# Pairing the levels of a gated recurrence: two levels per step in column halves of one PSUM bank

## The chip, the cores and the metric

The kernel runs on one core of a Trainium2 chip. Its five engines each follow their own instruction stream: TensorE (PE; its weight loads are listed apart as PEld), VectorE (DVE), ScalarE (ACT), GpSimd (POOL) and SyncE (SP), which here only issues transfers. Streams are tied together by semaphores. The metric is device time in microseconds; lower is better.

## The reference, cut to what matters

Two model blocks run one after the other on a sequence of 512 tokens and width 2048. The second one has two branches that are computed side by side: a "rw" branch with 16 heads of 64, and a gated "hg" branch with 8 heads of 128. The change is in the gated branch, and a small part of it in the rw branch. Per head of the gated branch:

```python
b = jnp.cumsum(lf_c, axis=1)
diff = b[:, :, None] - b[:, None, :]
decay = jnp.where(causal, jnp.exp(jnp.where(causal, diff, 0.0)), 0.0)
att = jnp.einsum('btshd,bshd->btsh', q_c[:, :, None] * decay, k_c)
o_intra = jnp.einsum('btsh,bshv->bthv', att, i_c)
o_inter = jnp.einsum('bthd,bhdv->bthv', q_c * jnp.exp(b), S)
```

`att[t, s]` is the sum over the 128 channels d of q[t, d] * k[s, d] * exp(b[t, d] - b[s, d]) for s <= t: a causal product whose decay depends on the channel.

## The kernel before, in words

**Levels.** The kernel works in chunks of 128 tokens, 4 chunks for 512 tokens. The decay is made safe by levels: level lv (0 to 6) covers the pairs (t, s) whose positions differ first in bit lv, with t in the odd and s in the even half of a block of 2^(lv+1) tokens. For each level the reference point is the last token of the even half. `level_in` (VectorE, two operations) subtracts, `level_exp` (ScalarE) exponentiates, `level_mix` (VectorE, two operations, L1866 and L1867) multiplies the odd halves by q and the even halves by k into the buffer `mix[lv % 2]`. The product of that buffer with its own odd columns, 4 matmuls (one a chunk) of 128 channels, up to 128 output partitions and 64 columns (L1428), gives the level's part of `att`. It goes to PSUM bank 7, and a masked copy on VectorE (`keep_where`, L1251) takes it to `att` in SBUF. The eighth product, `hk` with `hqs` with 128 columns, gives the diagonal. After each copy the next product may overwrite the bank.

**Rows.** `level_rows` leaves away weight columns at the end that no pair needs: 127, 126, 124, 120, 114, 98, 66 for levels 0 to 6, and 128 for the diagonal.

**The order of the work.** Every engine walks through the same blocks of weights. A block is 8 slots (of 2 x 128 rows of the weights), a slot 8 points, and at each point TensorE does three products with 512 columns, which are the large matrix products (L281 to L283 where the weights are the stationary side, L285 to L287 in the output projection). ScalarE (L576) and VectorE (L744) split each slot's weights into a high and a low part, two slots ahead. The steps of the two branches are hung up at points: `hg_at(h, m)` gives the point of step m of head h, `rw_at(u, k)` that of the rw branch. Steps of heads 0 to 5 are 4.5 points apart, those of head 6 are 2.3 and those of head 7 are 2.0. TensorE runs a step exactly at its point; ScalarE and VectorE run those of a slot's first half before the split and those of the second half after it.

**Steps of the gated branch.** Steps 0 to 6 prepare q, k, the decay sums and the first two levels. At step m from 7 to 13 VectorE mixes level m - 7, and from 7 to 11 prepares level m - 5; from step 8 to 15 TensorE multiplies level m - 8 (step 15: the diagonal) and VectorE, after its mix, copies the product out. Step 17 turns `hkd`, steps 18 to 21 go through the chunks, 24 turns the output.

**Bank 7.** `D_USES` says which steps of the two branches use bank 7 and how many releases each needs; they are numbered in program order. `d_claim` makes TensorE wait until all earlier uses are released (semaphore `d_free`), `d_wait` makes the reader wait for the product (`d_done`). The rw branch uses it too, for four products a unit, among them the turn of its output (L1292, step END + 3).

**The rw branch.** It inverts triangular matrices of 128 in levels too. In levels 4 and 5 a step multiplies in quadrants of 64 x 64 (`level_halves_pe`): W (L1378) and T (L1381), 16 matmuls each, the two diagonal quadrants in turn. Their results for T are copied with a mask by VectorE in `chunk_dve`. The last level has T in the form of L1397.

fp32 matmuls appear in the trace as two records each, so 4 matmuls are x8. The first attention, far ahead of these branches, has products of 128 input partitions with 64 output partitions in two column halves (L338); they are named below as rows of the trace.

## Time and profile before

| | us |
|---|---|
| median of 3 runs | 3055.62 (3054.82 to 3061.11) |
| the profiled execution | 3057.21 |
| its span | 3055.1 |
| TensorE busy | 2950.8 |
| VectorE busy | 1702.6 |
| ScalarE busy | 1187.0 |

The span is the time from the first to the last instruction; the execution's own time has some 2 us around it. "Busy" of TensorE counts overlapping records once. A row of the timeline gives the start and the time to the last end of a run of like instructions; as matmuls overlap, what a group costs TensorE is read from the starts of its neighbours. An idle time is given in brackets with what ended it. The granted clock is a share of 2.4 GHz: 1.00, or 0.50 for 1.2 GHz.

### The profile page before, as it was taken

To read this page: it belongs to the slowest core of one execution; us is meant where nothing else is said; L and a number is where in the kernel's file an instruction comes from. 1 tells how busy PE (TensorE), PEld (TensorE's weight loads), DVE (VectorE), ACT (ScalarE), POOL (GpSimd) and SP (SyncE) were. 2 spreads that over 40 slices of the span, in tenths; PEclk is the share of its full clock that TensorE was granted. 3 is DMA by queue.
4 is the path that set the end of the run, shared out by engine and by line. 5 is a ranking of instruction groups with operands and counts; after the bars stand their busy time and mean duration, and the time that the engine had idled before them with its cause. 6 is when DMAs were issued, how large, how long until landed. Compare 5 with 4: busy or idle time off the path is not lost.

```text
span 3055.1 us, 40093 instructions
## 1 busy us (share of the span) xinstructions
PE 2950.8 (97%) x15738; PEld 2359.3 (77%) x15738; DVE 1702.6 (56%) x2961; ACT 1187.0 (39%) x2099; POOL 285.5 (9%) x517
## 2 busy tenths in 40 slices
PE   8999999999999999999999999999999999999897
PEld 6778777787878887777778877777777877867686
DVE  6554555545453336566653365657666666565647
ACT  5444343434332323333333333434544343434412
POOL 0110101001000000000000002202022020212001
PEclk9999999999999999999999999999999999999899
DMA  4222222222233322222233322212222131225334
GB/s 167 76 83 80 80 83 83 76 83 77 83 121 135 122 92 70 77 70 75 71 123 138 117 86 82 82 66 92 75 73 92 63 99 59 89 77 153 125 132 157
DMA packets 86010, 289.02 MB, mean 95 GB/s; under 512 B 12208, under 2 KB 12720, under 8 KB 85568
## 3 DMA queue, kind: packets, MB, share of 16 engines
q1 hardware_dynamic: 69696, 243.65, 23.4%
q0 software_dynamic: 16128, 42.81, 4.5%
q8 instruction: 127, 2.08, 0.3%
q14 instruction: 59, 0.48, 0.1%
HBM read 261.11 MB, written 25.17 MB: 94 GB/s over the span
## 4 chain that ended last, share of the span: by engine, by line
PE 81%; DVE 10%; ACT 4%; issue 3%; DMA 1%; POOL 1%; DVEq 0%; SPq 0%; ACTq 0%; POOLq 0%
PE bank L281 14%; PE bank L283 14%; PE bank L282 14%; PE bank L285 8%; PE bank L287 7%; PE bank L286 7%; PE bank L1428 2%; DVE mc_split L744 1%; ACT mc_split L576 1%; PE bank L338 1%; PE bank L318 1%; PE bank L1309 1%; PE bank L480 1%; PE bank L503 1%; PE bank L308 1%
## 5 line engine op out<-in xcount | busy, mean ns | idle before, releaser
L281 PE MATMUL bank<-ma_split,mc_split 128*128 128x512 f32 x2304 | 957.5, 416 | 13.3 <-DVE ma_split L902 8.4
L744 DVE TENSOR_TENSOR mc_split<-mc,mc_split 128x1024 fp32r<-128x1024 f32 x434 | 535.1, 1234 | 771.4 <-ACT mc_split L576 768.8
L283 PE MATMUL bank<-ma_split,mc_split 128*128 128x512 f32 x2304 | 905.4, 393 | 0.0
L282 PE MATMUL bank<-ma_split,mc_split 128*128 128x512 f32 x2304 | 902.6, 392 | 0.0
L576 ACT ACTIVATE mc_split<-mc 128x1024 fp32r<-128x1024 f32 x434 | 457.8, 1056 | 670.8 <-PE bank L285 357.0
L281 PEld LDWEIGHTS bank<-ma_split,mc_split 128*128 128x128 f32 x2304 | 436.5, 189 | 123.7 <-issue 50.0
L283 PEld LDWEIGHTS bank<-ma_split,mc_split 128*128 128x128 f32 x2304 | 434.4, 189 | 96.6
L282 PEld LDWEIGHTS bank<-ma_split,mc_split 128*128 128x128 f32 x2304 | 436.9, 190 | 78.7 <-issue 4.4
L285 PE MATMUL bank<-mc_split,ma_split 128*128 128x512 f32 x576 | 230.6, 400 | 5.0 <-DVE mb L1848 3.4
L287 PE MATMUL bank<-mc_split,ma_split 128*128 128x512 f32 x576 | 225.6, 392 | 0.0
L286 PE MATMUL bank<-mc_split,ma_split 128*128 128x512 f32 x576 | 225.3, 391 | 0.0
L285 PE MATMUL bank<-mc_split,mb_split 128*128 128x512 f32 x512 | 202.8, 396 | 2.4 <-DVE mc L986 2.4
L287 PE MATMUL bank<-mc_split,mb_split 128*128 128x512 f32 x512 | 200.1, 391 | 0.0
L286 PE MATMUL bank<-mc_split,mb_split 128*128 128x512 f32 x512 | 199.8, 390 | 0.0
L585 ACT ACTIVATE mc<-bank,stat 128x128 f32<-128x128 f32 (+3 forms) x128 | 67.6, 528 | 286.3 <-DVE stat L752 286.1
L285 PEld LDWEIGHTS bank<-mc_split,ma_split 128*128 128x128 f32 x576 | 108.9, 189 | 27.3 <-issue 6.6
L287 PEld LDWEIGHTS bank<-mc_split,ma_split 128*128 128x128 f32 x576 | 108.7, 189 | 23.3
L286 PEld LDWEIGHTS bank<-mc_split,ma_split 128*128 128x128 f32 x576 | 108.9, 189 | 20.7
L1251 DVE COPY_PREDICATED mc<-tril,bank 128x256 f32<-128x256 uint8 (+1 forms) x176 | 88.0, 548 | 52.3 <-PE bank L1309 27.8
L285 PEld LDWEIGHTS bank<-mc_split,mb_split 128*128 128x128 f32 x512 | 96.6, 189 | 22.2 <-issue 3.3
L287 PEld LDWEIGHTS bank<-mc_split,mb_split 128*128 128x128 f32 x512 | 96.4, 188 | 20.6
L286 PEld LDWEIGHTS bank<-mc_split,mb_split 128*128 128x128 f32 x512 | 96.7, 189 | 19.2
(370 smaller groups left out, 3516.7 us busy)
## 6 DMA issues: line engine op xcount, KB each, us to landing
mc<-in_w SPq DMA_DIRECT2D x434, 512.0 KB, 3.3
x<-mc POOLq DMA_DIRECT2D x8, 1024.0 KB, 5.0
y<-mb_split SPq DMA_DIRECT2D x28, 256.0 KB, 2.5
ma_split<-y POOLq DMA_DIRECT2D x28, 256.0 KB, 4.4
mb<-in_xt SPq DMA_DIRECT2D x8, 512.0 KB, 9.9
mc<-in_x POOLq DMA_DIRECT2D x4, 1024.0 KB, 5.5
mc<-x POOLq DMA_DIRECT2D x4, 1024.0 KB, 6.3
mats<-mc POOLq DMA_DIRECT2D x32, 128.0 KB, 2.2
```

Source lines behind the costliest of these rows:

```text
L281: mm = pe.matmul(banks[j][:], wh[:, c], act_hi[:, kt, :], start=(kt == 0), stop=False)
L282: pe.matmul(banks[j][:], wl[:, c], act_hi[:, kt, :], start=False, stop=False)
L283: last = pe.matmul(banks[j][:], wh[:, c], act_lo[:, kt, :], start=False, stop=(kt == KT - 1))
L285: mm = pe.matmul(banks[j][:], act_hi[:, kt, c], wh, start=(kt == 0), stop=False)
L286: pe.matmul(banks[j][:], act_hi[:, kt, c], wl, start=False, stop=False)
L287: last = pe.matmul(banks[j][:], act_lo[:, kt, c], wh, start=False, stop=(kt == KT - 1))
L308: pe.matmul(bank[:, 0:w], q_both[:, e, b * P:(b + 1) * P], k_twice[:, e, 0:w], start=True, stop=False)
L576: act.activation(w_high[:, s % NH, :, :], w_raw[:, s % NR, :, :], ACT.Copy).then_inc(w_hi, 1)
L585: act.activation(prob[:, n % 2, 0:nk], S_BANK[n % 2][:, 0:nk], ACT.Exp, bias=nmax[:, k:k + 1], accum_out=rsum[:, k:k + 1]).then_inc(p_exp, 1)
L744: dve.tensor_tensor(w_low[:, s % NR, :, :], w_raw[:, s % NR, :, :], w_high[:, s % NH, :, :].bitcast(F32), ALU.subtract).then_inc(w_lo, 1)
L1251: return dve.copy_predicated(to, mask, frm)
L1428: mm = pe.matmul(to[0:rows, c], lhs[:, c * P:c * P + rows], frm[:, c], start=True, stop=True)
```

## The change

Six of the seven levels are handled in pairs, at steps 9, 11 and 13 (`HG_PAIRS`). Both levels of a pair are multiplied in one step into one bank: each level has 128 columns of it, 32 for each of 4 chunks, and its upper and lower 64 tokens stand on the upper and lower 64 partitions. So each chunk of a level is two matmuls, one to a column half of the array, with at most 64 weight columns and 32 moving columns. The diagonal comes at step 9 with levels 0 and 1, in two halves of 64 x 64 a chunk, in the bank's other 256 columns. The last level (6) stays alone in the old form, at step 14. Nothing uses the bank at steps 8, 10, 12 and 15.

The mixes are issued in pairs (`HG_MIX`), with the following pair's `level_in` and exponentials behind them (`HG_NEXT`): levels 0 and 1 at step 7, 2 and 3 at step 9, 4 and 5 at 11, 6 at 13. At steps 9, 11 and 13 VectorE first copies the products out, now two copies a level (one for each half), then mixes. The copies of the second level of a pair wait for the release that the first level's copy of the same half gave, and so do those of the diagonal.

`half_level_rows` leaves away weight columns in a half: 63, 62, 60, 56, 48 and 34 for levels 0 to 5. The T products of the rw branch use it as well, and so do their copies: 48 and 34 output partitions instead of 64 in levels 4 and 5.

```diff
             D_USES = {("rw", k): 1 for k in (0, 1, 2, END + 3)}
-            D_USES |= {("hg", m): 1 for m in (0, *range(8, 16), 17, 24)} | {("hg", m): 1 + (m < 21) for m in range(18, 22)}
+            HG_PAIRS = {9: (0, 1), 11: (2, 3), 13: (4, 5)}
+            HG_DIAG = 9
+            HG_MIX = {7: (0, 1), 9: (2, 3), 11: (4, 5), 13: (6,)}
+            HG_NEXT = {7: (2, 3), 9: (4, 5), 11: (6,)}
+            D_USES |= {("hg", m): 4 + 2 * (m == HG_DIAG) for m in HG_PAIRS}
+            D_USES |= {("hg", m): 1 for m in (0, 14, 17, 24)} | {("hg", m): 1 + (m < 21) for m in range(18, 22)}
...
+            def half_level_rows(lv):
+                return HD if lv >= LEVELS else HD - (1 << lv) + 2 * (lv == LEVELS - 2)
+            def half_cols(x, lv, half):
+                n = HD >> (lv + 1)
+                return halves(four(x), lv)[1][:, :, half * n:(half + 1) * n, :]
+            def pair_bank(lv, half):
+                at = P * (lv % 2)
+                return D_BANK[half_rows(half), at:at + P].rearrange("p (q n t) -> p q n t", q=NCH, t=1 << lv)
+            def diag_bank(half):
+                return four(D_BANK[half_rows(half), 2 * P:4 * P])
...
-                            mm = pe.matmul(out, xw[rows, q, half * HD:(half + 1) * HD], in_half(xt, lv, half, 1)[:, q],
+                            n = half_level_rows(lv)
+                            mm = pe.matmul(out[0:n], xw[rows, q, half_rows(half, n)], in_half(xt, lv, half, 1)[:, q],
                                            start=True, stop=True)
...
-                if 8 <= m < 16:
-                    lv = m - 8
-                    if lv < LEVELS:
-                        pe.wait_ge(h_mix, 14 * h + 2 * lv + 2)
-                    lhs, rhs = (mix[lv % 2], mix[lv % 2]) if lv < LEVELS else (hk, hqs)
...
+                if m in HG_PAIRS:
+                    pe.wait_ge(h_mix, 14 * h + 2 * HG_PAIRS[m][-1] + 2)
+                    for lv in HG_PAIRS[m]:
+                        for c in range(NCH):
+                            for half in range(2):
+                                to, frm = pair_bank(lv, half)[:, c], half_cols(mix[lv % 2], lv, half)[:, c]
+                                n = half_level_rows(lv)
+                                mm = pe.matmul(to[0:n], four(mix[lv % 2])[:, c, half_rows(half, n)], frm, start=True, stop=True)
+                    if m == HG_DIAG:
+                        for c in range(NCH):
+                            for half in range(2):
+                                mm = pe.matmul(diag_bank(half)[:, c], four(hk)[:, c, half_rows(half)],
+                                               four(hqs)[:, c, half_rows(half)], start=True, stop=True)
+                    mm.then_inc(d_done, 1)
...
-                if 7 <= m < 12:
-                    level_exp(act, h, m - 5)
+                for lv in HG_NEXT.get(m, ()):
+                    level_exp(act, h, lv)
...
-                if 7 <= m < 14:
-                    level_mix(dve, m - 7, h)
-                if 7 <= m < 12:
-                    level_in(dve, m - 5, h)
-                if 8 <= m < 16:
+                if m in HG_PAIRS:
                     d_wait(dve, "hg", h, m)
...
+                    taken = D_BEFORE["hg", h, m]
+                    for lv in HG_PAIRS[m]:
+                        for half in range(2):
+                            n = half_level_rows(lv)
+                            if lv % 2:
+                                dve.wait_ge(d_free, taken + half + 1)
+                            mask = in_half(lmaskt[:, lv:lv + 1, :], lv, half, 1)[0:n]
+                            keep_where(dve, in_half(att, lv, half, 1)[0:n], mask.broadcast_to([n, NCH, *mask.shape[2:]]),
+                                       pair_bank(lv, half)[0:n]).then_inc(d_free, 1)
...
+                for lv in HG_MIX.get(m, ()):
+                    level_mix(dve, lv, h)
+                for lv in HG_NEXT.get(m, ()):
+                    level_in(dve, lv, h)
```

On TensorE, in the last head (inside the output projection, whose products are L285 to L287), the program before has a level after every 6 weight products and the rw branch's turn (L1292) between levels 1 and 2:

```order
L1428 MATMUL bank<-mb 127x64 x4
...
L1428 MATMUL bank<-mb 126x32x2 x4
...
L1292 MATMUL bank<-ident,mb 128x128 x4
...
L1428 MATMUL bank<-mb 124x16x4 x4
...
L1428 MATMUL bank<-mb 120x8x8 x4
...
L1428 MATMUL bank<-mb 114x4x16 x4
```

The changed program at the same place, where L1448 is a level in halves, L1452 the diagonal and L1314 the same turn:

```order
L1448 MATMUL bank<-mb 63x32 x8
L1448 MATMUL bank<-mb 62x32 x8
L1452 MATMUL bank<-mb 64x64 x8
L285 MATMUL bank<-mc_split,ma_split 128x512
L286 MATMUL bank<-mc_split,ma_split 128x512
L287 MATMUL bank<-mc_split,ma_split 128x512
L1314 MATMUL bank<-ident,mb 128x128 x4
...
L1448 MATMUL bank<-mb 60x32 x8
L1448 MATMUL bank<-mb 56x32 x8
```

Three products stand together ahead of the turn, and 12 weight products lie between one group and the next, three of them ahead of the turn.

On VectorE, in the same head, the first four steps with levels read before (L1866 and L1867 are a mix, L1859 and L1860 a `level_in`, L1794 and L1795 belong to the rw branch):

```order
L1866 TENSOR_TENSOR mb<-mb 128x256
L1867 TENSOR_TENSOR mb<-mb 128x256
L1859 TENSOR_TENSOR mb<-mb 128x64x4
L1860 TENSOR_TENSOR mb<-mb 128x64x4
L1794 RECIPROCAL mb<-mb 128x8
L1795 TENSOR_TENSOR mb<-mb 128x512
L1866 TENSOR_TENSOR mb<-mb 128x128x2
L1867 TENSOR_TENSOR mb<-mb 128x128x2
L1859 TENSOR_TENSOR mb<-mb 128x32x8
L1860 TENSOR_TENSOR mb<-mb 128x32x8
L1251 COPY_PREDICATED mb<-lmaskt,bank 127x256
```

And in the changed program (L1900 and L1901 a mix, L1893 and L1894 a `level_in`, L1273 the copies):

```order
L1900 TENSOR_TENSOR mb<-mb 128x256
L1901 TENSOR_TENSOR mb<-mb 128x256
L1900 TENSOR_TENSOR mb<-mb 128x128x2
L1901 TENSOR_TENSOR mb<-mb 128x128x2
...
L1827 RECIPROCAL mb<-mb 128x8
L1828 TENSOR_TENSOR mb<-mb 128x512
L1273 COPY_PREDICATED mb<-lmaskt,bank 63x4x32 x2
L1273 COPY_PREDICATED mb<-lmaskt,bank 62x4x16x2 x2
L1273 COPY_PREDICATED mb<-lmaskt,bank 64x4x64 x2
L1900 TENSOR_TENSOR mb<-mb 128x64x4
```

The second mix now directly follows the first, ahead of the rw branch's operations and of both `level_in`, and six copies stand ahead of the next pair's mixes.

## Rows read from the trace of the kernel before

**Rows 1.** The page: busy us of an engine, share of the span, instructions

```profile
PE 2950.8 (97%) x15738; PEld 2359.3 (77%) x15738; DVE 1702.6 (56%) x2961; ACT 1187.0 (39%) x2099; POOL 285.5 (9%) x517
```

**Rows 2.** Waits of TensorE, 1950 to 3060 us: us in total, times, longest

```profile
PE bank L1428 <- DVE mb L1867: 13.8, 2, 7.4
PE bank L1428 <- DVE mb L1251: 6.7, 6, 3.0
PE bank L1405 <- DVE mc L1840: 6.5, 3, 2.7
...
PE bank L1292 <- DVE mb L1251: 0.5, 1, 0.5
```

**Rows 3.** Timeline of TensorE, levels 0 and 6 of head 3: start, us, work

```profile
2365.89 0.99 PE L1428 MATMUL bank<-mb 128*127 128x64 f32 x8
2366.69 0.48 PE L281 MATMUL bank<-ma_split,mc_split 128*128 128x512 f32 x1
2367.01 0.39 PE L282 MATMUL bank<-ma_split,mc_split 128*128 128x512 f32 x1
2367.24 0.40 PE L283 MATMUL bank<-ma_split,mc_split 128*128 128x512 f32 x1
...
2397.65 0.64 PE L1428 MATMUL bank<-mb 128*66 128x64 f32 x8
2398.10 0.48 PE L281 MATMUL bank<-ma_split,mc_split 128*128 128x512 f32 x1
2398.42 0.39 PE L282 MATMUL bank<-ma_split,mc_split 128*128 128x512 f32 x1
```

**Rows 4.** Timeline of TensorE, quadrant products of the rw branch

```profile
2383.29 0.39 PE L283 MATMUL bank<-ma_split,mc_split 128*128 128x512 f32 x1
2383.61 1.12 PE L1381 MATMUL bank<-mc 64*64 64x32 f32 x32
2384.66 0.50 PE L281 MATMUL bank<-ma_split,mc_split 128*128 128x512 f32 x1
2385.00 0.39 PE L282 MATMUL bank<-ma_split,mc_split 128*128 128x512 f32 x1
...
2398.98 1.14 PE L1395 MATMUL bank<-mc 64*64 64x64 f32 x16
2400.05 0.66 PE L1408 MATMUL bank<-mc 128*128 128x64 f32 x4
```

**Rows 5.** Timeline of TensorE: L338 in column halves, L1272 on the full array

```profile
330.82 2.37 PE L338 MATMUL bank<-mc 128*64 128x512 f32 x16
...
2145.51 1.12 PE L1272 MATMUL bank<-mb,small 128*128 128x512 f32 x2
...
2146.70 0.39 PE L282 MATMUL bank<-ma_split,mc_split 128*128 128x512 f32 x1
```

**Rows 6.** One line's view of L338: records, ns min/median/max, start us, forms

```profile
L338 PE MATMUL bank<-mc x256: 272/432/643, 121.1 to 887.7; 128*64 128x512 f32 x32, 128*64 128x384 f32 x32, 128*64 128x256 f32 x32, 128*64 128x128 f32 x32
```

**Rows 7.** Timeline of TensorE: the diagonal of head 0, level 0 of head 7

```profile
1991.74 2.07 PE L1428 MATMUL bank<-mb 128*128 128x128 f32 x8 [3.03 <-DVE mb L1251]
...
2859.28 1.94 PE L1428 MATMUL bank<-mb 128*127 128x64 f32 x8 [7.42 <-DVE mb L1867]
```

**Rows 8.** Stretches: us, busy of each engine, granted clock of TensorE, DMA

```profile
1991.60:1995.00 3.40, 3.26 (x12) 2.98 (x13) 2.24 (x4) 0.00 (x0) 0.00 (x0) 0.50 0.00 0
2859.00:2863.00 4.00, 3.72 (x13) 3.36 (x14) 3.90 (x11) 2.95 (x5) 0.00 (x0) 0.50 0.00 0
```

**Rows 9.** Groups of VectorE by form: count, busy us, mean ns, idle before

```profile
L1867 DVE TENSOR_TENSOR mb<-mb 128x256 f32<-128x256 f32 x56 | 24.4, 435 | 0.0
...
L1251 DVE COPY_PREDICATED mb<-lmaskt,bank 128x512 f32<-128x512 uint8 x8 | 5.8, 730 | 7.5 <-PE bank L1428 7.4
...
L1251 DVE COPY_PREDICATED mb<-lmaskt,bank 127x256 f32<-127x256 uint8 x8 | 5.8, 725 | 0.0
...
L1251 DVE COPY_PREDICATED mb<-lmaskt,bank 124x256 f32<-124x256 uint8 x8 | 3.4, 431 | 2.0 <-PE bank L1428 2.0
```

More of the change, by code:

```diff
@@ L1417, in hg_pe @@
                     turn4(pe, D_BANK, hi_).then_inc(d_done, 1)
[L1418 to L1425 removed]
+                if m in HG_PAIRS:
[12 more added lines that the diff above has]
+                    mm.then_inc(d_done, 1)
+                if m == 14:
+                    lv = LEVELS - 1
+                    rows = level_rows(lv)
+                    pe.wait_ge(h_mix, 14 * h + 2 * lv + 2)
+                    to, frm = halves(four(D_BANK[:]), lv)[1], halves(four(mix[lv % 2]), lv)[1]
                     for c in range(NCH):
[L1427 to L1428 removed]
+                        mm = pe.matmul(to[0:rows, c], mix[lv % 2][:, c * P:c * P + rows], frm[:, c], start=True, stop=True)
                     mm.then_inc(d_done, 1)
```

30 lines of the change are left out of this document (16 added, 14 removed).

## The prediction

> **What bounds the kernel now.** I read the page first, then the waits of TensorE in the second half, the timeline of TensorE around single groups, and the clock by stretches.
>
> The page shows TensorE busy for 2950.8 of 3055.1 us and VectorE for 56% [rows 1]: time can only come from what TensorE executes or waits for. The waits of the second half [rows 2] say where the gated branch makes it wait. Twice, 13.8 us in all, the first level product waits for the first mix (L1867). Six times, 6.7 us in all, a level product waits for VectorE to empty the one shared bank (L1251 before L1428); the longest, 3.03 us, is before the diagonal product of head 0 [rows 7]. The 6.5 us at L1405 belong to the other branch, and no edit touches them.
>
> What a level costs without waiting is read from the starts. A group of 8 records (4 matmuls in plain fp32, two records each) with 127 weight columns holds the next weight product up by 2366.69 - 2365.89 = 0.80 us, and the step from that product to its neighbour is 0.32 instead of 0.23, so 0.89 in all; with 66 columns it is 0.45 + 0.09 = 0.54 [rows 3]. Between them that is 0.00574 us a column and 0.161 a group. The eight steps of a head have 127, 126, 124, 120, 114, 98, 66 and 128 columns, together 903: 8 x 0.161 + 903 x 0.00574 = 6.47 us a head, 51.8 us for 8 heads.
>
> **The level products, paired and in halves.** Removed per head: six groups of levels and one diagonal group. Added: three groups of 48, 32 and 32 records (8 matmuls a level, 64 output partitions at most, 32 moving columns; the diagonal 8 matmuls with 64). The last level stays as it is, 0.54. In total 120 records instead of 64, so everything hangs on whether the two column halves run side by side.
>
> The trace has two neighbours. In the other branch, 32 records on two quadrants take 2383.61 to 2384.66, 1.05 us, while 16 records on one quadrant take 2398.98 to 2400.05, 1.07 us [rows 4]: two tiles work at the price of one. Those quadrants also differ in input partitions, which column halves don't. The column halves of the first attention (L338: 128 input partitions, 64 output partitions, as the new products) are the nearer case: a quarter of the records each with 512, 384, 256 and 128 columns, 16 in a group [rows 6], 4 x 1280 = 5120 columns. They take 2.37 us to the last one's end. Two fp32 records of 512 columns on the full array hold up the product after next by 2146.70 - 2145.51 = 1.19, less its own 0.23, 0.96 us for 1024 columns; 5120 would be 4.8 us one after the other [rows 5]. So column halves overlap, and I take it for the new groups. Per tile I count 0.45 / 8 = 0.056 us a record (66 columns, rows 3). A tiled group costs 1.05 - 16 x 0.056 = 0.15 of filling and 0.09 + 0.11 at its edges [rows 4], 0.35 in all. With 24, 16 and 16 records a tile: 1.69 + 1.25 + 1.25 + 0.54 = 4.73 a head. Saved: 1.74 a head, **13.9 us**. The bounds: by serial halves, 112 x 0.056 + 3 x 0.35 + 0.54 = 7.86, a loss of 1.39 a head or 11.1 us; by a load that shrinks with its columns (next part), 3.4 us more gain.
>
> **The trimmed products.** The weights lose 1 to 30 of 64 columns (387 instead of 448 over a head's seven pairs), and two steps of the other branch go from 64 to 48 and 34. If a record's time follows its weight columns as in rows 3, the level groups give 8 x 61 x 0.056 / 64 = 0.43 a head (3.4 us), and the other branch 16 x 46 x 0.056 / 64 = 0.64 a unit (5.2 us). The trace has no record with under 64 weight columns and a short stream, so this is open between 0 and 8.6. Rows 4 have the same time for 32 and for 64 moving columns, so something other than the stream sets 0.056 to 0.066; it may be the load or a floor per instruction. I take **0**, since no row shows a record that comes faster than that, and keep 8.6 for the range.
>
> The Trainium skill (TensorEngine Tiling (Array Packing), Instruction Overhead) says that a matmul has some 60 cycles of overhead and that one with a free dimension of 1 has the latency of one with 60. By it the trim gives nothing, as rows 4 can be read; by the slope of rows 3 it gives the 8.6 us of the next case.
>
> **The shared bank.** One bank now holds two levels and, at step 9, the diagonal; it is claimed four times a head instead of eight. The wait at level 1 (step 9 for step 8's copy) loses its cause, since step 9 needs only mixes issued at step 7. The diagonal's wait at step 15 goes with the step. These are the 6.7 us. What is late next? After the last level the next claim is the turn at step 17, 9 points on (27 weight products, 6.2 us at 0.23), or one of the other branch's, some 10 points on. That covers the 3.03 us. I take **5.5** (0 to 6.7). Head 0 gives more: behind its wait the granted clock is 0.50 for 3.4 us, the level of 1.2 GHz, and the 8 records of the diagonal last 2.07 [rows 7, 8]. Without the wait these 3.4 us hold work of 1.7: **1.7** (0 to 1.7).
>
> **Heads 6 and 7.** Their steps stand 2.3 and 2.0 points apart. TensorE reaches the first step with a mix 6.4 and 7.4 us early, and then works at 0.50 of the clock [rows 2, 7, 8]. The first claim moves from step 8 to step 9, two points later: 6 weight products, 1.4 us. But it needs the second mix as well: 0.8 us of VectorE in two operations of 435 ns [rows 9], behind its exponential on ScalarE. So at most 0.6 goes per head. Against it, the 48 records of step 9 fall into the slow clock as a block: 3.4 us instead of 1.7. Before, levels 0 and 1 did, some 3.5 instead of 1.8 (1.94 for level 0) [rows 7]. About equal. In head 7 the other branch's turn at L1292 follows step 9 after 3 weight products and claims the same bank. It waits 0.5 now for one copy [rows 2]; it will wait for six, about 2.0 us less the 0.7 of those products, 1.3: 0.8 more. Step 14 follows 13 after 6 products in head 7 (1.4 us), and VectorE must make four copies and a mix in between, 1.1 + 0.8: 0.5 more. But this head's diagonal and four edges are gone from step 15 on and nothing waits there. I take **0.8** for both, with -4 to +3.
>
> **VectorE and ScalarE.** Copies now: 0.725 (level 0, and level 1 alike), 0.431 (from level 2) and 0.730 for the diagonal [rows 9]. From 256 to 512 elements the price rises by 0.30, so 128 elements cost some 0.28, twice a level: 0.13 more on each of six levels, 0.8 us a head, 6 us on an engine that is busy for 56% [rows 1]. It costs nothing where TensorE is 9 points from the next step (6.2 us for some 2.0 of copies and 1.7 of mixes). That cover is gone in heads 6 and 7, where it is counted. The split of weights (L744) comes later in the pair order, since ScalarE runs two exponentials before its half of it. It works two slots ahead, 16 points or 48 products of 0.23, 11 us, so I cost it at nothing; without that cover each late split would stop TensorE.
>
> **The sum.** 13.9 + 0 + 5.5 + 1.7 + 0.8 = 21.9 us. The profiled execution took 3057.21 us (span 3055.1 and 2.1 around it), 1.6 above the median 3055.62. 3057.21 - 21.9 = 3035.3 against that execution, 3033.7 against the median: **3034 us**.
>
> **Rivals.**
> 1. *The trim pays.* A record's time follows its weight columns below 64 too, as it does above in rows 3. 8.6 us more: 3025. For it: the slope from 127 to 66 columns. Against it: rows 4.
> 2. *The handoff to VectorE eats half.* Four or six copies and two mixes stand between TensorE's groups; TensorE waits at steps 11, 13 and 14 and at L1292, in heads 6 and 7 above all, and the clock falls again. The 5.5 come back as later waits and 5 more are lost: 3044. For it: 13.8 us of waits there already. Against it: six of eight heads have 6 us between steps.
> 3. *All of it comes back*, by waits of the other branch whose VectorE work doesn't get earlier: the 6.5 us at L1405 would have to grow by 21.9, to four times their size. 3055, no change.
> 4. *The halves run one after the other* (slower). The column halves share their 128 input partitions, and with 32 columns there is little stream to hide a load behind, unlike L338's. It decides from 0.053 us a record in sequence: 112 x 0.053 + 1.59 is 7.5 a head, 1.0 more than 6.47, and 8.0 in all eats the other three terms; side by side it would be 0.028. Then +11.1, less 5.5 + 1.7, plus 2 for longer groups in the slow clock of heads 6 and 7: +6 to +8, 3062. Against it: rows 5, whose last quarter has only 128 columns.
>
> The Trainium skill (TensorEngine Tiling (Array Packing), Restrictions) says that column tiling switches fast weight load off, which speaks for rival 4. The trace doesn't bear it out: the halves of L338 overlap all the same [rows 5].
>
> **The numbers.** Forecast 46%, rival 1 26%, rival 2 16%, rival 3 6%, rival 4 6%. The forecast's own range is 3029 to 3039. For 8 in 10 it reaches down to all trims and 6.7 of waits with 3 in the last heads (3021), and up to rival 2 with a little more (3046). About 0.2%, 6 us, is what a measurement of this kernel tells from no change. Faster by more: 88%; within: 6%; slower: 6%.
>
> **What the changed profile would show.** The three tiled groups of a head between weight products: 1.7, 1.25 and 1.25 us if I am right, 1.6, 1.1 and 0.9 in rival 1, about 3.0, 2.1 and 2.1 in rival 4. The T products of the other branch: 1.05 us still, or less. No wait at the diagonal, no half clock near 1992 us. The first waits of heads 6 and 7 near 6 and 7 us; L1292's near 1.3. The forecast is wrong if waits of TensorE before the new groups exceed 5 us outside heads 6 and 7, or if a tiled group costs over 2.5.

## The result and the profile after

The changed kernel takes 3071.89 us, the median of 6 runs (3068.36 to 3076.16), against 3055.81 for the kernel before beside it: a ratio of 1.0046, 95% interval 1.0036 to 1.0055. It is slower by some 14 to 16 us, where the prediction said 22 faster. The loss is in the order of the work: two small edits of order, each alone, bring the changed kernel to 3047 and 3048, and a version without pairs reaches 3031 (below).

The profiled execution, the longest of the six, has a span of 3074.1 us, so the traces show 19.0 us of loss where the medians show 16. The page's row of busy time, which answers to [rows 1]:

```profile
PE 2947.8 (96%) x16186; PEld 2344.1 (76%) x16186; DVE 1714.0 (56%) x3017; ACT 1186.2 (39%) x2099; POOL 279.8 (9%) x517
```

TensorE is busy for 3.0 us less and idle for 22.0 more (3074.1 - 2947.8 = 126.3, against 104.3). Its own work did shrink. The timeline of TensorE at steps 9, 11 and 13 of head 3, and two T products of the rw branch with 48 and 34 weight columns (start us, us, work), the answer to [rows 3, 4]:

```profile
2366.45 0.39 PE L283 MATMUL bank<-ma_split,mc_split 128*128 128x512 f32 x1
2366.77 1.10 PE L1448 MATMUL bank<-mb 128*63 128x32 f32 x32
2367.71 0.66 PE L1452 MATMUL bank<-mb 128*64 128x64 f32 x16
2368.30 0.50 PE L281 MATMUL bank<-ma_split,mc_split 128*128 128x512 f32 x1
...
2377.75 1.04 PE L1448 MATMUL bank<-mb 128*60 128x32 f32 x32
2378.73 0.50 PE L281 MATMUL bank<-ma_split,mc_split 128*128 128x512 f32 x1
...
2392.71 0.82 PE L1448 MATMUL bank<-mb 128*48 128x32 f32 x32
2393.46 0.50 PE L281 MATMUL bank<-ma_split,mc_split 128*128 128x512 f32 x1
...
2004.00 0.91 PE L1404 MATMUL bank<-mc 64*48 64x32 f32 x32
2004.84 0.55 PE L1280 MATMUL bank<-ident,mb 128*128 128x128 f32 x3
...
2013.57 0.72 PE L1404 MATMUL bank<-mc 64*34 64x32 f32 x32
2014.22 0.50 PE L281 MATMUL bank<-ma_split,mc_split 128*128 128x512 f32 x1
```

From its start to that of the next weight product, the three groups take 1.53, 0.98 and 0.75 us; with 0.20 for the edges of each (the prediction's figure) that is 1.73, 1.18 and 0.95. With 0.54 for the last level that is 4.40 us a head where it was 6.47: 16.6 us over 8 heads. The T products take 0.84 and 0.65 instead of 1.05: 0.61 a unit, 4.9 us. So TensorE has 21.5 us less to do.

What used up this gain stands in two views. First the waits of TensorE from 1950 to 3080 us (us in total, times, longest), the answer to [rows 2]:

```profile
PE bank L1448 <- DVE mb L1901: 13.0, 2, 6.7
PE bank L1387 <- DVE mc L1273: 7.8, 5, 3.0
PE bank L1404 <- ACT mc L1595: 6.6, 2, 3.6
PE bank L1428 <- DVE mc L1874: 6.5, 3, 2.7
PE bank L281 <- DVE mb L1719: 6.4, 5, 2.6
...
PE bank L1400 <- ACT mc L1595: 4.4, 4, 2.8
...
PE bank L1448 <- ACT mb L1573: 2.4, 1, 2.4
...
PE bank L1314 <- DVE mb L1273: 1.4, 1, 1.4
```

The waits of level products for VectorE's copies out of the shared bank are gone, as forecast. One wait for that bank has grown, from 0.2 to 2.4 us: in head 7 the pair of step 11 waits until ScalarE has read the rw branch's turn out of it (L1573). Most of the new waits are in the other branch, rw: its W and T products (L1400, L1404) wait for ScalarE's evictions (L1595), and its turns (L1387) for VectorE's copies of T (L1273). Second the clock: in the records of granted clock 20 stretches, 111.5 us in all, are at half (1.2 GHz), where it was 11 stretches and 72.4 us. The last stretch of each, 16.3 and 14.6 us, stands at the end, where TensorE has no more work. Within the stretches TensorE is busy for 88.6 us where it was 45.7. So 43.0 us more are spent at half pace, on work of 21.5 at full pace: as much as was saved. Its busy time moved by -3.0, so these sizes are good to some 3 us.

One place shows how the waits arise. The timeline of the changed kernel in head 4, from step 9 on; TensorE, VectorE and ScalarE (in brackets the idle time before, and what ended it):

```profile
2501.96 1.11 PE L1448 MATMUL bank<-mb 128*63 128x32 f32 x32
2502.89 0.67 PE L1452 MATMUL bank<-mb 128*64 128x64 f32 x16
...
2504.38 1.12 PE L1400 MATMUL bank<-mc 64*64 64x32 f32 x32
...
2510.74 1.49 PE L1404 MATMUL bank<-mc 64*48 64x32 f32 x32 [2.98 <-ACT mc L1595]
...
2503.71 2.80 DVE L1273 COPY_PREDICATED mb<-lmaskt,bank 63x128 f32<-63x128 uint8 x6 [3.35 <-PE bank L1452]
2506.54 0.43 DVE L1900 TENSOR_TENSOR mb<-mb 128x256 f32<-128x256 f32 x1
...
2508.23 0.42 DVE L1894 TENSOR_TENSOR mb<-mb 128x256 f32<-128x256 f32 x1
...
2508.68 1.30 ACT L1652 ACTIVATE mb<-mb 128x512 f32<-128x512 f32 x2 [6.71 <-DVE mb L1894]
2509.89 0.80 ACT L1595 ACTIVATE mc<-bank 64x256 f32<-64x256 f32 x2
2510.71 1.06 ACT L576 ACTIVATE mc_split<-mc 128x1024 fp32r<-128x1024 f32 x1
```

The same eviction in the kernel before (its line is L1562 there):

```profile
2504.80 0.82 ACT L1562 ACTIVATE mc<-bank 64x256 f32<-64x256 f32 x2 [2.21 <-PE bank L1378]
2505.64 1.06 ACT L576 ACTIVATE mc_split<-mc 128x1024 fp32r<-128x1024 f32 x1
```

The W product is done near 2505.5. Before, ScalarE emptied its bank at once. Now ScalarE's queue has the exponentials of levels 4 and 5 (L1652) ahead of the eviction. They wait for VectorE's level inputs (L1894), and VectorE makes six copies and four mix operations first. So ScalarE stands idle for 6.71 us, and the eviction starts at 2509.89, over 4 us after its product is done. TensorE stands for 2.98 us, and then works at half clock. The windows view, in which the granted clock is the last value but two, shows this stretch and the next, and one in head 0 just ahead of the place of that in [rows 8]:

```profile
2510.60:2517.40 6.80, 6.66 (x49) 5.70 (x50) 2.25 (x3) 2.14 (x4) 0.00 (x0) 0.50 0.01 2
2527.60:2537.80 10.20, 9.29 (x40) 7.10 (x40) 0.82 (x2) 2.76 (x6) 0.00 (x0) 0.50 0.14 53
...
1984.90:1991.70 6.80, 6.29 (x21) 5.06 (x22) 6.63 (x9) 1.06 (x1) 0.00 (x0) 0.50 0.22 77
```

The wait for the bank in head 7 (L1573, above) has the same cause. The turn that L1573 reads is done near 2884.3; ahead of L1573 stand two exponentials, which wait for VectorE, and a split:

```profile
2885.72 1.30 ACT L1652 ACTIVATE mb<-mb 128x512 f32<-128x512 f32 x2 [6.00 <-DVE mb L1894]
2886.93 1.04 ACT L576 ACTIVATE mc_split<-mc 128x1024 fp32r<-128x1024 f32 x1
2887.87 0.76 ACT L1573 ACTIVATE mb<-bank,mc 128x512 f32<-128x512 f32 x1
```

Over the whole run ScalarE's waits for the level inputs, of the kernel before and of the changed one:

```profile
ACT mb L1619 <- DVE mb L1860: 79.2, 47, 4.2
```

```profile
ACT mb L1652 <- DVE mb L1894: 120.2, 39, 9.8
```

By the same weight product in both traces, the changed kernel is still 1.9 us ahead at 2338 us, before the levels of head 3, and then loses some 3, 9, 7 and 2 us in heads 3 to 6, where the rw branch's and the gated branch's steps fall together.

### The profile page after: what moved, and what is told of

It is laid out like the page before. It is cut to its first block, busy times and chain, and to the rows that moved or that the text cites. A ratio compares the mean times of both kernels' runs of the same rounds, so it can differ in the third digit from the quotient of the medians.

```text
span 3074.1 us, 41077 instructions
## 1 busy us (share of the span) xinstructions
PE 2947.8 (96%) x16186; PEld 2344.1 (76%) x16186; DVE 1714.0 (56%) x3017; ACT 1186.2 (39%) x2099; POOL 279.8 (9%) x517
## 4 chain that ended last, share of the span: by engine, by line
PE 80%; DVE 11%; ACT 4%; issue 3%; DMA 1%; POOL 0%; DVEq 0%; SPq 0%; ACTq 0%; POOLq 0%
PE bank L281 15%; PE bank L283 14%; PE bank L282 14%; PE bank L285 7%; PE bank L287 7%; PE bank L286 7%; ACT mc_split L576 1%; PE bank L338 1%; DVE mc_split L744 1%; PE bank L318 1%; PE bank L1331 1%; DVE mb L1273 1%; PE bank L480 1%; PE bank L503 1%; PE bank L308 1%
## 5 line engine op out<-in xcount | busy, mean ns | idle before, releaser
L281 PE MATMUL bank<-ma_split,mc_split 128*128 128x512 f32 x2304 | 961.9, 418 | 17.1 <-DVE ma_split L902 7.3
L744 DVE TENSOR_TENSOR mc_split<-mc,mc_split 128x1024 fp32r<-128x1024 f32 x434 | 535.3, 1234 | 784.9 <-ACT mc_split L576 782.5
L281 PEld LDWEIGHTS bank<-ma_split,mc_split 128*128 128x128 f32 x2304 | 439.4, 191 | 131.1 <-issue 54.7
L285 PE MATMUL bank<-mc_split,ma_split 128*128 128x512 f32 x576 | 230.2, 400 | 5.0 <-DVE mb L1882 3.4
L287 PE MATMUL bank<-mc_split,ma_split 128*128 128x512 f32 x576 | 225.5, 392 | 0.0
L285 PE MATMUL bank<-mc_split,mb_split 128*128 128x512 f32 x512 | 202.8, 396 | 2.4 <-DVE mc L986 2.4
L287 PE MATMUL bank<-mc_split,mb_split 128*128 128x512 f32 x512 | 200.2, 391 | 0.0
L285 PEld LDWEIGHTS bank<-mc_split,ma_split 128*128 128x128 f32 x576 | 108.8, 189 | 27.9 <-issue 6.6
L287 PEld LDWEIGHTS bank<-mc_split,ma_split 128*128 128x128 f32 x576 | 108.5, 188 | 23.3
L1273 DVE COPY_PREDICATED mc<-tril,bank 128x256 f32<-128x256 uint8 (+1 forms) x176 | 88.1, 548 | 55.1 <-PE bank L1331 30.6
L285 PEld LDWEIGHTS bank<-mc_split,mb_split 128*128 128x128 f32 x512 | 96.5, 188 | 22.3 <-issue 3.3
L287 PEld LDWEIGHTS bank<-mc_split,mb_split 128*128 128x128 f32 x512 | 96.5, 188 | 20.5
```

The costliest lines, as they stand in the source:

```text
L281: mm = pe.matmul(banks[j][:], wh[:, c], act_hi[:, kt, :], start=(kt == 0), stop=False)
L285: mm = pe.matmul(banks[j][:], act_hi[:, kt, c], wh, start=(kt == 0), stop=False)
L287: last = pe.matmul(banks[j][:], act_lo[:, kt, c], wh, start=False, stop=(kt == KT - 1))
L744: dve.tensor_tensor(w_low[:, s % NR, :, :], w_raw[:, s % NR, :, :], w_high[:, s % NH, :, :].bitcast(F32), ALU.subtract).then_inc(w_lo, 1)
L1273: return dve.copy_predicated(to, mask, frm)
```

## The experiments

Two theories at first. **A**: the block is on ScalarE's queue; what stands behind the pair's two exponentials is late. **B**: VectorE is late by its copies, and all it hands on is late. Later experiments ask what is left after that. Each median is of 5 to 11 executions. "Idle" is TensorE's, the span less its busy time; "half" is the time at half clock, up to 0.4 us low by rounding and with the 13 to 16 us at the end. Both are of the one profiled execution.

| kernel | median us | ratio to before (95%) | span | idle | half |
|---|---|---|---|---|---|
| before | 3055.8 | 1 | 3055.1 | 104.3 | 72.4 |
| changed | 3071.9 | 1.0046 (1.0036-1.0055) | 3074.1 | 126.3 | 111.5 |
| e1 exponentials a step later | 3047.1 | 0.9966 (0.9952-0.9979) | 3045.3 | 110.9 | 78.1 |
| e2 copies last | 3048.0 | 0.9975 (0.9966-0.9985) | 3045.9 | 113.8 | 81.0 |
| e3 both | 3046.6 | 0.9969 (0.9956-0.9981) | 3046.7 | 113.2 | 84.4 |
| e4 trim of rw alone | 3053.2 | 0.9988 (0.9979-0.9997) | 3050.5 | 106.8 | 62.1 |
| e5 spread mixes | 3074.8 | 1.0051 (1.0039-1.0064) | 3071.7 | 131.8 | 97.1 |
| e6 halves, no pairs | 3046.6 | 0.9957 (0.9944-0.9971) | 3043.9 | 107.8 | 69.8 |
| e7 spread, exponentials later | 3045.9 | 0.9958 (0.9946-0.9971) | 3042.2 | 114.0 | 70.1 |
| e8 halves, diagonal at 9 | 3037.0 | 0.9932 (0.9919-0.9944) | 3036.6 | 101.9 | 69.4 |
| e9 mixed schedule | 3045.1 | 0.9957 (0.9945-0.9969) | 3040.6 | 109.1 | 71.4 |
| e10 last pair only | 3040.0 | 0.9944 (0.9932-0.9957) | 3038.9 | 105.9 | 68.7 |
| e11 as e8, exponentials later | 3030.7 | 0.9918 (0.9905-0.9932) | 3027.8 | 99.0 | 58.6 |
| e12 before, exponentials later | 3054.5 | 0.9987 (0.9978-0.9996) | 3052.5 | 101.7 | 69.0 |

The kernel before had medians of 3055.8 to 3060.9 beside these, so compare by the ratio.

**e1, exponentials a step later.** The edit, in ScalarE's function:

```diff
-                for lv in HG_NEXT.get(m, ()):
+                for lv in HG_NEXT.get(m - 1, ()):
                     level_exp(act, h, lv)
```

> The changed kernel with one edit: ScalarE issues the exponentials of a pair of levels (L1652) one step later (steps 8, 10, 12 of a head instead of 7, 9, 11), behind the evictions of the rw branch that share the step. Theory A (head of line on ScalarE: the two exponentials of the next pair wait for VectorE, which first does six copies and four mixes, and what stands behind them, the evictions L1595 and the split of the weights L576, L744, comes up to 7 us late; TensorE then waits and falls to half clock): the waits of TensorE on L1595 in 1950 to 3080 us (6.6 + 4.4 + 1.2 = 12.2 us) go to under 3, half-clock time falls from 111.5 us towards the 72.4 of before, ScalarE's idle in front of L1652 falls from 120.2 us below 60, and the time is 3035 to 3050. Theory B (VectorE itself is late by its six copies, and everything it hands on is late whatever ScalarE does): waits on L1273 (7.8 + 2.8 + 2.3 + 1.4 = 14.3 us) stay, half-clock time stays over 100 us, and the time is 3065 to 3073.

Measured: 3047.1. The eviction of head 4's W product follows its product again, and the waits on L1595 fall from 12.2 us to 1.7. Timeline of ScalarE in e1, and two lines of TensorE's waits:

```profile
2499.08 0.82 ACT L1595 ACTIVATE mc<-bank 64x256 f32<-64x256 f32 x2 [3.56 <-PE bank L1400]
2499.92 1.06 ACT L576 ACTIVATE mc_split<-mc 128x1024 fp32r<-128x1024 f32 x1
2502.24 1.31 ACT L1652 ACTIVATE mb<-mb 128x512 f32<-128x512 f32 x2 [1.25 <-DVE mb L1894]
```

```profile
PE bank L1387 <- DVE mc L1273: 7.5, 8, 1.5
...
PE bank L1400 <- ACT mc L1595: 0.5, 1, 0.5
```

No instruction of VectorE or TensorE was moved, so the 24 us came back by ScalarE's order alone: theory A holds for how the loss reaches TensorE, and B's 3065 to 3073 is refuted. Of B only the waits on L1273 are borne out: 12.3 us of its 14.3 are still there. The wait on L1573 is gone. ScalarE's idle in front of L1652 fell only to 73.3, not below 60.

**e2, copies last.** VectorE's mixes and level inputs of steps 9, 11 and 13 ahead of the copies:

```diff
                 if m in HG_PAIRS:
                     d_wait(dve, "hg", h, m)
+                for lv in HG_MIX.get(m, ()):
+                    level_mix(dve, lv, h)
+                for lv in HG_NEXT.get(m, ()):
+                    level_in(dve, lv, h)
+                if m in HG_PAIRS:
                     taken = D_BEFORE["hg", h, m]
...
-                for lv in HG_MIX.get(m, ()):
-                    level_mix(dve, lv, h)
-                for lv in HG_NEXT.get(m, ()):
-                    level_in(dve, lv, h)
```

> The changed kernel with one edit: at steps 9, 11 and 13 VectorE does the mixes and the level inputs (L1900, L1893) before the copies of the pair (four or six, 440 ns and less each, some 2.8 us at step 9) instead of behind them; ScalarE's order is as in the changed kernel. Theory A (ScalarE's two exponentials block what is queued behind them): the block is shorter by the 2.8 us of copies, so the idle in front of L1652 falls from 120.2 us to about 120 - 7 x 4 = 90, part of the waits on L1595 goes, and the time is 3052 to 3064. Theory B (the copies make VectorE late for the level inputs): that is the whole lateness, and the time is 3035 to 3048.

Measured: 3048.0, which theory A missed (3052 to 3064) and which lies at the edge of B's range. ScalarE's standing fell from 120.2 us to 91.9, near A's 90, and the waits on L1595 from 12.2 to 2.3. So a shorter stand is enough to bring the time back as e1 did. The copies made the stand long, and ScalarE's order passed it on.

**e3, both edits**, that of e2 and

```diff
-                for lv in HG_NEXT.get(m, ()):
+                for lv in HG_NEXT.get(m - 1, ()):
```

> Both edits: the exponentials a step later on ScalarE, and VectorE's mixes and level inputs ahead of the copies. Theory A: as the first edit alone within 5 us (3032 to 3048), since the second only shortens a block that the first has taken away. Theory B: as the second edit alone. If both engines' orders are needed, it is over 8 us faster than either of them alone.

Measured: 3046.6, no more than either alone. It is one chain with two links, and breaking either is enough. About 20 us of the gain that TensorE's shorter work promises are still missing.

**e4, the trim of the rw branch alone**, on the kernel before: L1381's weights and output, and the copies' rows.

```diff
-                            mm = pe.matmul(out, xw[rows, q, half * HD:(half + 1) * HD], in_half(xt, lv, half, 1)[:, q],
+                            n = half_level_rows(lv)
+                            mm = pe.matmul(out[0:n], xw[rows, q, half_rows(half, n)], in_half(xt, lv, half, 1)[:, q],
```

> The kernel before with only the trimmed T products of the rw branch (L1381: weights and output of 63 to 34 columns instead of 64, and the copies of as many rows), levels one per step as before. In the changed kernel a group of these took 0.94 us at 48 columns and 0.75 at 34 against 1.15 at 64, 0.61 us of TensorE a unit. If what is saved reaches the end: 8 x 0.61 = 4.9 us, 3051. If TensorE's waits and clock take it back: 3055 to 3058. If the groups stay at 1.15 the shorter ones of the changed kernel had another cause.

Measured: 3053.2, a ratio of 0.9988 with 0.9979 to 0.9997, so 1 to 6 us. The trim pays. Its 4.9 lies within that, but is not told apart from 3. TensorE is busy for 7.1 us less and idle for 2.5 more.

**e5, mixes, level inputs and exponentials one level a step again**, pairs on TensorE untouched:

```diff
-            HG_MIX = {7: (0, 1), 9: (2, 3), 11: (4, 5), 13: (6,)}
-            HG_NEXT = {7: (2, 3), 9: (4, 5), 11: (6,)}
+            HG_MIX = {m: (m - 7,) for m in range(7, 14)}
+            HG_NEXT = {m: (m - 5,) for m in range(7, 12)}
```

> The changed kernel with TensorE's part untouched (pairs at steps 9, 11, 13, the diagonal at 9), but VectorE's mixes and level inputs and ScalarE's exponentials one level a step again, as in the kernel before (mix of level m-7 and input of level m-5 at step m; at steps 9, 11 and 13 behind the copies). Asked is what the remaining loss of the two repaired kernels is (3047 where the summed savings of TensorE would give about 3028). Theory C (the burst: eight tensor_tensor of VectorE in a row, 8 x 0.35 = 2.8 us, stand ahead of the split L744 and the copies L1273 of the T quadrants, so that L1387 waits about 1.2 us ten times): spreading takes the eight to two times four, the waits L1387<-L1273 fall from 7.5 us to under 3, and the time is 3034 to 3042. Theory D (the six and four copies themselves, or the loss lies at heads 6 and 7): the waits stay and the time is 3045 to 3050. If the block on ScalarE behind the copies is still there (its exponential of level 4 waits at step 9 for the same copies), L1595 waits again and it is 3050 to 3065.

Measured: 3074.8, as slow as the changed kernel and beyond the 3065 of the third case. ScalarE stands 135.0 us, 52 times, in front of its exponentials, since at step 9 even one level's input comes behind six copies. So spreading the mixes without the other edit says nothing on theory C, that the burst of eight operations in a row is what costs.

**e7, the same with the exponentials a step later**, the edit of e5 and

```diff
-                for lv in HG_NEXT.get(m, ()):
+                for lv in HG_NEXT.get(m - 1, ()):
```

> The spread order with the exponentials one step later on ScalarE as well. Theory A and C together: nothing of ScalarE stands any more behind an exponential that waits for VectorE's copies; at or under the spread order alone, 3032 to 3042. If the spread order alone was already free of the block it is the same within 2 us. An exponential a step later brings the mix of the next level closer to its product: where that decides, waits in front of L1448 outside heads 6 and 7 and 3045 to 3055.

Measured: 3045.9. With e5 this is the cleanest pair: one line of ScalarE's order is worth 29 us, on spread mixes as on paired ones. Theory C is right in its wait and not in its time: L1387 on L1273 is 3.8 us where e1 has 7.5, but L1448 on L1901 is 19.6 where e1 has 13.1, eight times instead of two, since a pair now waits for a mix issued one step before it.

**e6, halves without pairs.** One level a step at 8 to 13, the diagonal at 15, VectorE's order as before:

```diff
-            HG_PAIRS = {9: (0, 1), 11: (2, 3), 13: (4, 5)}
-            HG_DIAG = 9
+            HG_PAIRS = {**{m: (m - 8,) for m in range(8, 14)}, 15: ()}
+            HG_DIAG = 15
```

> Column halves and trimmed quadrants without pairs: one level a step at steps 8 to 14 and the diagonal at 15, everything on VectorE and ScalarE in the order of the kernel before, two half copies in place of one. TensorE keeps the shorter groups and pays the edges (about 0.2 us) of four more groups a head, 8 x 0.8 = 6 us against the pairs. If pairing is what costs (theory A and C): no new waits of the rw branch, 0.7 x 22 + 5 - 6 = about 17 to 20 us under before, 3036 to 3042. If the half copies on VectorE are what costs (theory B and D): 3045 to 3055.

Measured: 3046.6. No wait of the rw branch is new. It missed the 3036 to 3042: I had put the pairs' advantage at 0.8 us a head. From start to next start the single groups take 0.58 + 0.58 + 0.56 + 0.54 + 0.48 + 0.39 us and the diagonal 0.61; with 7 x 0.20 for edges and 0.54 for the last level that is 5.68, against 6.47 before and 4.40 in pairs. So 0.79 a head, 6.3 us, and 4.9 of the rw branch are saved, 11.2 in all, and the span is 11.2 shorter. That the two agree so well is in part luck: TensorE is busy for 14.7 us less and idle for 3.5 more. 1.28 a head, 10.2 us, are the pairs' own. That e1 to e3 are no faster than e6 for all that is the price of their waits: idle of 111 to 114 us against 108, and half clock of 78 to 84 against 70.

**e8, the same with the diagonal at step 9**, behind level 1:

```diff
-            HG_PAIRS = {**{m: (m - 8,) for m in range(8, 14)}, 15: ()}
-            HG_DIAG = 15
+            HG_PAIRS = {m: (m - 8,) for m in range(8, 14)}
+            HG_DIAG = 9
```

> Column halves, one level a step (as in the kernel without pairs), with one edit: the diagonal stands at step 9 behind level 1 instead of at step 15. Asked is the prediction's term for the waits in front of the diagonal (L1453 <- L1273 is 5.4 us in four heads there, with a half clock of 3.4 us behind the one of 3.03 us) and the edge of one group a head (8 x 0.2 = 1.6 us). If this term is real: 5.4 + 1.7 + 1.6 = 8.7 us under the kernel without pairs, a ratio to before near 0.993. If VectorE's two more half copies at step 9 (0.9 us) push the wait on (level 2 at step 10 waiting for copies, or a T copy late): the same as the kernel without pairs within 2 us, 0.9957.

Measured: 3037.0, 0.9932 where 0.993 was expected. In e6 the diagonal (L1453) waited for the bank, 5.4 us; in e8 that row is gone, and what is left of bank waits in front of a level is the second row here (waits of TensorE in e6, then in e8):

```profile
PE bank L1453 <- DVE mb L1273: 5.4, 4, 3.0
PE bank L1449 <- DVE mb L1273: 4.6, 5, 1.4
```

```profile
PE bank L1449 <- DVE mb L1902: 13.8, 2, 7.4
...
PE bank L1449 <- DVE mb L1273: 3.2, 3, 1.2
```

So the prediction's term for the diagonal's wait is real: TensorE is idle for 5.9 us less. Its term for the clock is not shown. The stretch of 3.4 us near 1993 is gone, but others have come elsewhere: half clock is 69.4 us against 69.8, and TensorE is busy for only 1.4 us less, the edge's 1.6. The ratios differ by 7.6 us, where 8.7 were expected.

**e9, pairs with a mixed schedule**: e7 in heads 0 to 5 and e1 in heads 6 and 7.

```diff
-            HG_MIX = {m: (m - 7,) for m in range(7, 14)}
-            HG_NEXT = {m: (m - 5,) for m in range(7, 12)}
+            HG_MIX = [{m: (m - 7,) for m in range(7, 14)}] * 6 + [{7: (0, 1), 9: (2, 3), 11: (4, 5), 13: (6,)}] * 2
+            HG_NEXT = [{m: (m - 5,) for m in range(7, 12)}] * 6 + [{7: (2, 3), 9: (4, 5), 11: (6,)}] * 2
```

> Pairs on TensorE with the exponentials a step later; mixes one level a step in heads 0 to 5 and both of a pair in heads 6 and 7. The spread order alone had 6.5 + 1.0 + 8.4 + 0.8 + 1.7 = 18.4 us in front of L1448 in heads 6 and 7 against 13.1 with both mixes in one step, and the latter had 4 us more of L1387 <- L1273 in heads 3 to 5. If both differences are separate costs, this takes the better of each: 4 to 6 us under the spread order with late exponentials, a ratio near 0.994. If TensorE's waits only move on (what heads 0 to 5 save is waited for later): 0.9957 as that one.

Measured: 3045.1, 0.9957, the same as e7 (0.9958). The waits on L1901 did fall, from 19.6 to 14.2, and the span by 1.6 only. The shorter waits did not make the kernel measurably faster.

**e10, the last pair only**: e8 with levels 4 and 5 as a pair at step 13.

```diff
-            HG_PAIRS = {m: (m - 8,) for m in range(8, 14)}
+            HG_PAIRS = {8: (0,), 9: (1,), 10: (2,), 11: (3,), 13: (4, 5)}
...
+                if m == 13:
+                    d_wait(dve, "hg", h, m)
                 for lv in HG_MIX.get(m, ()):
```

> The kernel with single levels and the diagonal at step 9, with one edit: levels 4 and 5 as a pair at step 13 (nothing of TensorE's at step 12); mixes, level inputs and exponentials stay one level a step in the old order, but the mix of level 6 at step 13 now waits for the pair's products. On TensorE a pair in place of two groups of 48 and 34 columns is 0.86 us in place of 0.57 + 0.48 + 2 x 0.11 = 1.27 with the edges, 0.3 to 0.4 us a head, 8 x 0.35 = 2.8 us. If pairing costs only where a handoff stands behind a wait (theory A), 2 to 3 us faster, a ratio near 0.9925; if the mix of level 6 behind the pair makes the last level wait (1 us a head and more), the same or slower, 0.993 to 0.997.

Measured: 3040.0, 0.9944 against 0.9932 of e8; the intervals overlap a little, and the last case (the same or slower) holds. The wait at the last level is only 0.6 us, though. By the same weight product, the 2.3 us by which this span is longer than e8's are there already after head 0. Timeline of e10 in head 0, VectorE and TensorE:

```profile
1983.96 0.42 DVE L1901 TENSOR_TENSOR mb<-mb 128x256 f32<-128x256 f32 x1 [3.58 <-PE bank L1449]
...
1984.75 1.29 DVE L1273 COPY_PREDICATED mb<-lmaskt,bank 48x128 f32<-48x128 uint8 x4
...
1986.07 1.23 DVE L744 TENSOR_TENSOR mc_split<-mc,mc_split 128x1024 fp32r<-128x1024 f32 x1
...
1987.35 1.89 DVE L1720 TENSOR_TENSOR mb<-bank,mc 128x512 f32<-128x512 f32 x3
1988.19 0.47 PE L281 MATMUL bank<-ma_split,mc_split 128*128 128x512 f32 x1 [1.34 <-DVE mb L1720]
```

The mix of level 6 must wait for the pair's products, since level 4 still uses its buffer. VectorE stands 3.58 us for it, then makes four copies and a split, and only then reads the bank of another product, the gates' (L1720), for which a weight product waits. The same row (L281 waiting for that read) is 4.7 us in all here, 4.6 in e1 and e9, 6.4 in the changed kernel, and 1.7 in the kernels without pairs. So VectorE's queue shows the same mechanism.

**e11, e8 with the exponentials a step later:**

```diff
-                for lv in HG_NEXT.get(m, ()):
+                for lv in HG_NEXT.get(m - 1, ()):
```

> The kernel with single levels and the diagonal at step 9, with the exponentials one step later on ScalarE. In the kernel before ScalarE stood 79 us in front of its exponentials (L1619), 47 times, at most 4.2 us, and no eviction was late by it. Theory A says that a short stand there is hidden: the same within 2 us, 0.993. If every us of standing counts, 3 to 8 us faster (0.991). If an exponential a step later makes the mixes of heads 6 and 7 late (as in the spread order), 2 to 5 us slower (0.994 to 0.995).

Measured: 3030.7, 0.9918: 4 to 6 us under e8, and the best of all. Half clock falls from 69.4 to 58.6 us, bank waits in front of levels from 3.2 to 1.0.

**e12, the kernel before with the exponentials a step later**:

```diff
-                if 7 <= m < 12:
-                    level_exp(act, h, m - 5)
+                if 8 <= m < 13:
+                    level_exp(act, h, m - 6)
```

> The kernel before with one edit: ScalarE issues each level's exponential (L1619) one step later (steps 8 to 12 of a head instead of 7 to 11). Nothing of TensorE's or VectorE's order changes. In the kernel with single levels and the diagonal at 9 this edit gave about 5 us. If the stand of ScalarE in front of these exponentials (79.2 us, 47 times, longest 4.2 us) already cost something in the kernel before, this is 3 to 8 us faster (3048 to 3053) and the prediction's sentence that ScalarE's order has room was wrong of the kernel before too; if it costs only with half copies, it is the same within 2 us.

Measured: 3054.5, 0.9987 with 0.9978 to 0.9996: 1 to 7 us, at the edge of what can be told. The stand of 79 us, now 40, cost a little already in the kernel before; its bank waits in front of levels are 4.7 us instead of 6.7. Where the rest of e11's gain comes from is open: part of its shift against e8 (2 us of the 8.8 in the spans) lies before the gated branch starts, where no edit acts.

## Why the prediction was wrong

**The failed step is the last paragraph of its change part, "VectorE and ScalarE".** It put the moved split at nothing, "since ScalarE runs two exponentials before its half of it", and the copies at nothing, since "TensorE is 9 points from the next step". It asked when TensorE comes to the next step of the gated branch, and when it needs the split. It did not ask what else stands in ScalarE's queue behind two exponentials that wait for VectorE. That is the eviction L1595, which TensorE needs soon: in the kernel before the T product started 2.2 us after the eviction did (2506.97 against 2504.80), where the split has 11. For the split itself the 11 us held: no weight product waits longer for it (L744), its row is 1.5 us before and after. But its late half on VectorE delayed the T copies behind it, as in the 2.98 us in front of L1387 in head 4. e1, and e7 against e5, show that this one order costs 24 to 29 us.

VectorE's block was counted too short as well. At step 9 of head 4 the six copies take 2.80 us, where 2.0 were forecast (those of levels 0 and 1 take 0.44 each, not 0.28), and the four mix and four level-input operations behind them 2.8 more, where the mixes alone were counted, 1.7. The prediction's own sign of being wrong, waits before the new groups outside heads 6 and 7, could not show this: there are none, since the loss is in the other branch.

**The level products.** 13.9 us were forecast, from 1.7, 1.25 and 1.25 us a group; measured are 1.73, 1.18 and 0.95. Column halves of one set of 128 input rows do overlap, as read from L338 [rows 5], and rival 4 (about 3.0, 2.1 and 2.1) is refuted. This overlap does not test what the prediction quotes on fast weight load; no run here shows whether that was on. The mechanism was right, the saving too small by the trim: 16.6 us.

**The trim** was taken as 0 with 8.6 as the other end. It is 0.33 x 8 = 2.6 us in the levels (4.73 less 4.40, with the untrimmed size as forecast) and 4.9 in the rw branch, 7.5 in all; rival 1 was right here. The reading of rows 4 was wrong: equal time for 32 and 64 moving columns does not say that a record has a floor in its weight columns too. At 32 moving columns a group shrinks from 1.05 to 0.65 us when only its weight columns go from 64 to 34. The Trainium skill (TensorEngine Tiling (Array Packing), Instruction Overhead) gives a free dimension of 1 the latency of one of 60. Read for the moving columns, that is in line with rows 4; carried over to the weight columns, as the prediction did, it is not what these runs show.

**The shared bank and the clock behind it.** No wait on L1273 in front of a level is left in the changed kernel, and the one at the diagonal of head 0 has gone with its half clock [rows 7, 8]. e8 finds the wait at its size, and not the 1.7 us of clock. In the changed kernel a stretch of half clock of 6.8 us, twice the old one, stands just ahead of the old place, behind a wait of 2.6 us (L281 for L1719). From step 14 to the turn at step 17 the code has 13 points, not the 9 of the prediction; nothing rests on it.

**Heads 6 and 7.** First waits 6.2 and 6.7 (forecast "near 6 and 7"), L1314 1.4 (forecast 1.3), the last level 0.8 (forecast 0.5). Not forecast: the 2.4 us at step 11 of head 7 for the bank, which ScalarE frees (L1573) behind the exponentials. That is the failed step again.

**The rivals.** The slower case had the wrong mechanism, and rival 2 (a handoff that eats half) looked for the waits at steps 11, 13 and 14 of the same branch. Rival 3 named the other branch, but its one wait (L1405, now L1428) stayed at 6.5 us. With the measured sizes the sum would have been 21.5 + 5.5 + 1.7 + 0.8, 3026; the gap to 3072 is 46 us. The order on ScalarE accounts for 25 (e1). The other 21 are idle time and clock. In e1 TensorE is idle for 6.6 us more than before, where 6.3 less were forecast; the largest new rows are L1387 on L1273 (7.5 us, none before) and L281 on L1719 (4.6, before 1.7). It is busy for 56.0 us in half-clock stretches, before 45.7: 5.2 us of work more, where 1.7 less was forecast. That this goes with the pairs is shown by the kernels without them. e8 has 8.6 us less saved by its groups than a pair kernel (one edge of 0.20 a head less than e6, so 5.48 against 4.40) and is 8 to 10 us faster than e1, e3 and e9. e11 has late exponentials, spread mixes and the copies behind them. It is 15 us faster than e7, which differs by the pairs and by copies ahead of the mixes, and 16 faster than e3, which differs by the pairs and by paired mixes. How the 21 divide among the waits is not settled.

## What to carry to other kernels

When a step hands more work at once to an in-order engine, look at every instruction queued behind the one that waits, of all branches, and at who waits for each: the time to the next step of the same branch is not the slack. Put an instruction that must wait for another engine behind what is ready to run, one step later if its consumer allows it. This one line was worth 24 us here, and 1 to 7 us in kernels where TensorE hardly waited for what stood behind it (e11, e12). A larger group saves TensorE its edges, but it hands its results on as one block, so try the smaller groups in the same form as well.

## What the runs showed of the hardware

- Groups of 32 records on two 64-row quadrants with 32 moving columns: 1.05 us with 64 weight columns, 0.84 with 48, 0.65 with 34. That is 0.0004 us per record and weight column (0.21 / (32 x 16) and 0.19 / (32 x 14)). From 32 to 64 moving columns no such effect is seen: 16 records a quadrant take 1.05 and 1.07 us [rows 4].
- Plain fp32 matmuls on two column halves with the same 128 input rows overlap down to 32 moving columns: the 16 records of level 0 hold the next weight product up by 0.58 us in e6. Where another tiled group follows, in the changed kernel, they take 0.48 us, 0.030 each; full-array records with 66 weight columns take 0.056 each [rows 3].
- From before to the changed kernel TensorE has 22.0 us more idle time, in waits of 1 to 4 us, and 43.0 us more of its busy time at half clock, work of 21.5 at full pace. So the short waits went with as large a loss again by the clock. Some stretches of half clock stand where no edit acts: one near 1426 us is there in e1, e8 and e10 and not in the others. So a few us of "half" differ without a cause in the kernel.
- Masked copies on VectorE of 128 elements from PSUM: 0.44 us each in levels 0 and 1 (63 and 62 partitions), 0.29 to 0.30 in levels 2 to 5. One copy of 256 elements took 0.725 and 0.431 before [rows 9], so two halves cost some 0.15 us more than one whole.
